# The norms between phases from three running sums, with GpSimd renewing half of the residual stream

## The chip, the cores and the metric

The kernel runs on one core of one Trainium2 chip. The metric is device time in microseconds (us) of the whole launch. The kernel before takes 2228.94 us, the median of 3 runs (2228.55 to 2229.42).

The engines by the names of the profile: PE is TensorE (PEld its weight loads), DVE is VectorE, ACT is ScalarE, POOL is GpSimd, SP is SyncE, which here only issues DMAs. A name with q behind it (SPq) is the queue of that engine.

## The reference

One inference step of a two-layer trunk over 384 tokens: 128 context tokens and 256 latent tokens (two groups with their own modulation vectors). Cut to what matters here:

```
def rmsnorm(x, g):
    xf = x * rsqrt(mean(x * x, axis=-1) + EPS)
    return xf * g

def trunk_layer(x, cond, ...):
    m = split(silu(cond) @ ada_w[l] + ada_b[l], 9)           # modulation, 9 x 1024
    h = rmsnorm(x, norm_pre[0]) * (1 + m[1]) + m[0]
    y = (silu(h @ wg) * (h @ wu)) @ wd                        # FFN, 1024 -> 2816 -> 1024
    x = x + 0.5 * m[2] * rmsnorm(y, norm_post[0])
    h = rmsnorm(x, norm_pre[1]) * (1 + m[4]) + m[3]
    y, _ = token_mixer(h, ...)                                # attention, recurrence, gates, @ w_out
    x = x + m[5] * rmsnorm(y, norm_post[1])
    h = rmsnorm(x, norm_pre[2]) * (1 + m[7]) + m[6]
    y = swiglu(h, ...)
    x = x + 0.5 * m[8] * rmsnorm(y, norm_post[2])
```

So between two products there are always two norms in a row: that of y (post), which makes the new x, and that of the new x (pre), which makes the next h. The places between are called gaps here. There are five of them inside the two layers, and one norm of y at the very end.

## The kernel before, in words

Everything is held with the 1024 features on the partitions, as 8 tiles (k = 0 to 7) of 128 features by 384 tokens, fp32. A sum over the features is therefore a product with a matrix of ones on PE (`ones`, the constant tile `con` in the rows), which leaves the sum of each token on all 128 partitions.

**Weights.** A unit is a block of 128x1024 fp32 weights (or 128x512). SP loads it into one of four `raw` slots (`stream`, L488). ACT copies it to `w_hi` (`highs`, L1028), POOL takes the rest of the rounding, `w_lo = raw - w_hi` (`lows`, L525, two instructions of 128x512), and PE does three products for each block: hi x hi, hi x lo, lo x hi (L588), 384 columns each. ACT and POOL work four units ahead of PE (SPLIT = 4). A `raw` slot is free for the next load when its low part is made; SP waits there in order (L485). A unit of kind "ada" (a slice of `ada_w`) is not split: PE multiplies it straight from the slot with the small `c_col` (`ada_unit`, L627).

**Phases.** A layer is up0, down0, gap0, proj and mixer, out, gap1, up1, down1, gap2. In a gap PE has up to 22 ada units to do (GAP = 22; the last gap, gap1 of layer 1, has 8). 18 of the 22 have places of their own (`hold_*`); numbers 14 to 17 go through the four `raw` slots, behind the first four weight units of the next phase. So number 17 is loaded when the low part of the fourth of these units is made. PE does all ada units of a gap before the first product of the next phase.

**The end of a phase.** y has four pairs of tiles, each pair in one PSUM pair X0 or X1. For each pair: ACT squares it (`y_square`, L1132, 128x768), DVE multiplies it by the column vector mG into `y` (`y_out`, L1601) and adds up the squares (L1606 to L1609).

**A gap.** PE sums the squares of y (`y_sums`, L696 to L699); ACT takes the square root (`root_of_sums`, L1088); DVE inverts it (L1560) and makes the new x in four steps (`post`: L1563 multiplies, L1565 and L1568 add); ACT squares each tile of x (L1110), PE sums them (`x_sums`, L705), ACT takes the root, DVE inverts it (L1538), and multiplies each tile (`pre`: L1527, L1532); ACT rounds to `h_hi` (L1117), DVE takes the rest, `h_lo` (`low`, L1518), and PE begins its products tile by tile (`by_tiles`).

Everything is ordered by semaphores that the code writes out by hand; each engine runs its instructions in the order of the code. There is no scheduler.

## Time and profile before

| | |
|---|---|
| time, median of 3 runs | 2228.94 us |
| the profiled execution, first to last instruction | 2228.5 us |
| PE busy | 2145.9 us (96%) |
| POOL busy | 1240.8 us (56%) |
| DVE busy | 915.8 us (41%) |
| ACT busy | 903.4 us (41%) |
| DMA | 311.37 MB, mean 140 GB/s |
| mean granted PE clock | 0.989 |

The profiled execution's own time is its span of 2228.5 us; 0.4 us separate it from the median, so what is worked out in one holds for the other. The page gives each group of instructions as: line, engine, operation, out<-in, shapes, count, busy us and mean ns of one, then the idle time before them and who ended it. A PE row of 0.33 us is one product whose next one starts 0.17 us later, since products are pipelined.

### The profile page before, as it was taken

Reading aid. Unit: us, or ns where it says so; the run is one execution under the profiler, and the core shown is the slowest. Engines: PE = TensorE matmul, PEld = TensorE weight load, DVE = VectorE, ACT = ScalarE, POOL = GpSimd, SP = SyncE. Lnnn points to the kernel's source line nnn. Section 1 sums busy time; section 2 is a strip of 40 time slices with the busy share of each in tenths; the row PEclk is TensorE's granted clock in tenths of the full one; section 3 lists DMA queues with packets and bytes.
Section 4 is the critical chain, followed back from the end, with each engine's and each line's share of the span. In section 5 each row is a group of like instructions: output and inputs, shape, how many; then the busy total and the mean of one; then the engine's idle time right before and its main releaser. Section 6 shows DMA issues by size and latency. Waiting matters only on the chain.

```text
span 2228.5 us, 32128 instructions
## 1 busy us (share of the span) xinstructions
PE 2145.9 (96%) x13212; PEld 2022.6 (91%) x13212; DVE 915.8 (41%) x1486; ACT 903.4 (41%) x1269; POOL 1240.8 (56%) x972
## 2 busy tenths in 40 slices
PE   6999999999899999999999999999999899899998
PEld 4999997988898988999979999799888899799997
DVE  5122116446766465121251221534576664622122
ACT  3222323246765534223243232324567546432332
POOL 2666553444478464666646666354435955366663
PEclk8999999999999999999999999999999999899999
DMA  7555674433222384445554446552322235244431
GB/s 282 160 163 172 224 237 162 124 88 95 67 86 86 109 297 117 129 133 171 193 185 124 138 124 234 194 152 87 87 78 76 86 114 176 61 136 128 124 123 67
DMA packets 306921, 311.37 MB, mean 140 GB/s; under 512 B 9923, under 2 KB 285655, under 8 KB 306775
## 3 DMA queue, kind: packets, MB, share of 16 engines
q1 hardware_dynamic: 299671, 303.55, 43.4%
q10 hardware_dynamic: 7104, 5.77, 0.8%
q8 instruction: 104, 1.70, 0.3%
q14 instruction: 42, 0.34, 0.1%
HBM read 305.35 MB, written 3.93 MB: 139 GB/s over the span
## 4 chain that ended last, share of the span: by engine, by line
PE 73%; DVE 12%; ACT 8%; POOL 3%; issue 2%; DMA 1%; SPq 0%; DVEq 0%; ACTq 0%
PE X L588 56%; PE S L588 6%; PE Ab L588 4%; POOL w_lo L525 2%; PE S L705 1%; ACT w_hi L1028 1%; POOL dec L553 1%; POOL dec L552 1%; PE X L766 1%; PE S L795 1%; ACT p L1181 1%; DVE mg_lo L1453 1%; DVE gate_b L1464 1%; PE X L848 1%; DVE root L1560 1%
## 5 line engine op out<-in xcount | busy, mean ns | idle before, releaser
L525 POOL TENSOR_TENSOR w_lo<-raw,w_hi 128x512 fp32r<-128x512 f32 (+1 forms) x872 | 1163.6, 1356 | 947.2 <-ACT w_hi L1028 938.2
L1028 ACT ACTIVATE w_hi<-raw 128x1024 fp32r<-128x1024 f32 (+1 forms) x436 | 453.3, 1041 | 723.6 <-PE X L588 687.7
L588 PE MATMUL X<-h_hi,w_hi 128*128 128x384 f32 x1600 | 539.7, 337 | 12.6 <-DVE h_lo L1518 12.6
L588 PE MATMUL X<-h_lo,w_hi 128*128 128x384 f32 x1600 | 536.8, 335 | 0.0
L588 PE MATMUL X<-h_hi,w_lo 128*128 128x384 f32 x1600 | 536.6, 335 | 0.0
L588 PEld LDWEIGHTS X<-h_hi,w_hi 128*128 128x128 f32 x1600 | 302.0, 189 | 24.5 <-DVE h_lo L1518 15.9
L588 PEld LDWEIGHTS X<-h_lo,w_hi 128*128 128x128 f32 x1600 | 302.0, 189 | 0.0
L588 PEld LDWEIGHTS X<-h_hi,w_lo 128*128 128x128 f32 x1600 | 301.9, 189 | 0.0
L1590 DVE TENSOR_TENSOR prod<-X,silu 128x768 f32<-128x768 f32 x44 | 42.1, 957 | 566.7 <-PE X L588 566.7
L588 PE MATMUL X<-act_hi,w_hi 128*128 128x384 f32 x704 | 236.4, 336 | 0.0
L588 PE MATMUL X<-act_hi,w_lo 128*128 128x384 f32 x704 | 235.3, 334 | 0.0
L588 PE MATMUL X<-act_lo,w_hi 128*128 128x384 f32 x704 | 235.3, 334 | 0.0
L1601 DVE TENSOR_SCALAR y<-X,mG 128x128 f32<-128x128 f32 x96 | 33.5, 411 | 340.7 <-ACT prod L1132 340.7
L588 PE MATMUL S<-h_hi,w_hi 128*128 128x384 f32 x480 | 166.5, 347 | 0.4 <-DVE proj L1432 0.4
L588 PE MATMUL S<-h_lo,w_hi 128*128 128x384 f32 x480 | 161.4, 336 | 0.0
L588 PE MATMUL S<-h_hi,w_lo 128*128 128x384 f32 x480 | 161.2, 336 | 0.0
L588 PEld LDWEIGHTS X<-act_hi,w_hi 128*128 128x128 f32 x704 | 132.1, 188 | 4.5 <-issue 4.5
L588 PEld LDWEIGHTS X<-act_lo,w_hi 128*128 128x128 f32 x704 | 132.2, 188 | 0.0
L588 PEld LDWEIGHTS X<-act_hi,w_lo 128*128 128x128 f32 x704 | 132.2, 188 | 0.0
L588 PE MATMUL Ab<-h_hi,w_hi 128*128 128x384 f32 x320 | 111.7, 349 | 0.7 <-DVE acc_e L1440 0.7
L588 PE MATMUL Ab<-h_hi,w_lo 128*128 128x384 f32 x320 | 107.3, 335 | 0.0
L588 PE MATMUL Ab<-h_lo,w_hi 128*128 128x384 f32 x320 | 107.2, 335 | 0.0
(364 smaller groups left out, 3075.3 us busy)
## 6 DMA issues: line engine op xcount, KB each, us to landing
raw<-in_w_in SPq DMA_DIRECT2D x124, 512.0 KB, 3.8
raw<-in_ffn_gate SPq DMA_DIRECT2D x88, 512.0 KB, 3.8
raw<-in_ffn_up SPq DMA_DIRECT2D x88, 512.0 KB, 3.7
raw<-in_ffn_down SPq DMA_DIRECT2D x80, 512.0 KB, 3.5
raw<-in_ada_w SPq DMA_DIRECT2D x48, 512.0 KB, 3.9
hold<-in_ada_w SPq DMA_DIRECT2D x29, 512.0 KB, 5.2
first_w<-in_ada_w SPq DMA_DIRECT2D x16, 512.0 KB, 10.6
hold_a<-in_ada_w SPq DMA_DIRECT2D x16, 512.0 KB, 6.4
```

Source lines behind the costliest of these rows:

```text
L525: ins = nc.gpsimd.tensor_tensor(slot(w_lo, u)[:, part], raw_of(u)[:, part], slot(w_hi, u)[:, part], SUB)
L552: nc.gpsimd.tensor_tensor(dst[:, :, 0:b], mid, src[:, :, 0:b], SUB)
L553: nc.gpsimd.tensor_tensor(dst[:, :, b:], src[:, :, b:], mid, SUB).then_inc(S["dec_ready"], 1)
L588: mm = nc.tensor.matmul(dst, w[:, k, m * 128:m * 128 + 128], r_, start=start and k + j == 0, stop=stop and k == u.nk - 1 and j == 2)
L705: mm = nc.tensor.matmul(S5[:, 0:T], ones, sq[:, k, :], start=k == 0, stop=k == KT - 1)
L766: mm = nc.tensor.matmul(X[n % 2][:, c, at_:at_ + k.shape[-1]], proj[64 * c:64 * c + 64, (AQ if kind == "a" else CQ) + h, b * 128:b * 128 + ...
L795: mm = nc.tensor.matmul((S5, S6)[c][:, 0:128], v, pT[:, c, j * 128:j * 128 + 128], start=j == 0, stop=j == len(kbs) - 1)
L848: mm = nc.tensor.matmul(X[0][:, j // 3, j % 3 * 128:j % 3 * 128 + 128], lev_k[n % 2][:, t], lev_q[n % 2][:, t], start=True, stop=True)
L1028: A(slot(w_hi, u), raw_of(u), ACT.Copy).then_inc(hi_ready[u.split], 1)
L1181: e = A(p[n % 2][:, c, 0:w], X[n % 2][:, c, 0:w], ACT.Exp, bias=nmax[:, n % 2, c:c + 1], accum_out=esum[:, n % 2, c:c + 1])
L1590: V.tensor_tensor(prod[:, :, :], X[1][:, :, 0:T], silu[:, :, :], MUL).then_inc(x_free[1], 1)
L1601: ins = V.tensor_scalar(y[:, 2 * i + m, t0:t1], X[u.dest][:, m, t0:t1], mG[:, 2 * i + m, g:g + 1], None, MUL)
```

## The change

While a phase's y tiles come out of PE, three sums over the features are built up instead of one: of the squares of the raw y (a), of x times the scaled y called g (b), and of the squares of g (c). With r = 1/sqrt(a/1024 + eps), the sum of the squares of the new x = x + r g is the old sum of x squared, plus 2 r b, plus r r c. So the norm of the new x is known before the new x is. The old sum is kept in `x_sum`.

- **Phase end**: `y_squares` (ACT) and `y_out` (DVE) go tile by tile: ACT squares the tile from PSUM, DVE makes g, ACT squares g, DVE multiplies x by g, adds that product to `y_sum`, and adds both squares to `silu[:, 0:2]` (one instruction of 768). The next tile's square on ACT waits for that last addition (`y_added`). The last pair is taken half by half (`half_done`).
- **Gap on PE**: three ada units, then three sums with ada units between them, then the rest of the ada units, then the products.
- **Gap on ACT**: an inverse root is now Ln and Exp (with a load of the function table between) in place of Sqrt on ACT and the reciprocal on DVE.
- **Gap on DVE**: `joint` makes the new `x_sum` in five dependent instructions, renews x tiles 0, 3, 6 and 7, and makes each normed tile with one instruction per token group (x times mA times the inverse root) where there were two.
- **Gap on POOL**: `add_to_x` renews x tiles 1, 2, 4 and 5 (four multiplications and four additions of 128x384). The high and low part of the fourth weight unit of the next phase, which stood before the gap, now stand behind: on ACT behind the first inverse root, on POOL behind `add_to_x`.
- At the start and at the very end the inverse root or root is Ln and Exp too.

```diff
@@ block.gpsimd
+            def add_to_x():
+                pool.wait_ge(S["root_ready"], 2 * seen.next("gap"))
+                for n, k in enumerate((*POOL_TILES, None)):
+                    if k is not None:
+                        nc.gpsimd.tensor_tensor(y[:, k, :], y[:, k, :], root[:, :], MUL).then_inc(S["y_pool_ready"], 1)
+                    if n:
+                        k = POOL_TILES[n - 1]
+                        pool.wait_ge(S["y_pool_ready"], seen.next("y_pool_ready"))
+                        nc.gpsimd.tensor_tensor(x[:, k, :], x[:, k, :], y[:, k, :], ADD).then_inc(S["x_pool_ready"], 1)
...
-                for f in range(2):
-                    lows(END[L, f"down{f}"] + SPLIT)
...
+                lows(END[L, "down0"] + SPLIT - 1)
+                add_to_x()
+                lows(END[L, "proj"] + SPLIT)
@@ block.tensor
             def gap(units):
-                y_sums()
-                early = 12 if len(units) > 12 else len(units) // 2
-                for u in units[:early]:
+                for u in units[:3]:
                     ada_unit(u)
-                x_sums([])
-                for u in units[early:]:
+                part_sum(S5[:, 0:T], silu[:, 0, :]).then_inc(S["sum_ready"], 1)
+                ada_unit(units[3])
+                pe.wait_ge(x_free[0], seen.value(("xf", 0)) + 1)
+                part_sum(X[0][:, 0, 0:T], y_sum[:, :])
+                ada_unit(units[4])
+                part_sum(X[0][:, 1, 0:T], silu[:, 1, :]).then_inc(S["sum_ready"], 1)
+                for u in units[5:]:
                     ada_unit(u)
@@ block.scalar
-            def root_of_sums():
+            def root_of_sums(power):
                 act.wait_ge(S["sum_ready"], seen.next("sum_ready"))
-                A(root[:, :], S5[:, 0:T], ACT.Sqrt, bias=eps[:, 0:1], scale=1.0 / D).then_inc(S["root_ready"], 1)
+                A(root[:, :], S5[:, 0:T], ACT.Ln, bias=eps[:, 0:1], scale=1.0 / D).then_inc(S["act_step"], 1)
+                act.wait_ge(S["act_step"], seen.next("act_step"))
+                A(root[:, :], root[:, :], ACT.Exp, scale=power).then_inc(S["root_ready"], 1)
...
+                        A(prod[:, 0, :] if k else silu[:, 0, :], X[u.dest][:, m, 0:T], ACT.Square).then_inc(S["y_sq_ready"], 1)
+                            act.wait_ge(S["g_made"], seen.next("g_made"))
+                            A(prod[:, 1, :] if k else silu[:, 1, :], y[:, k, :], ACT.Square).then_inc(S["c_made"], 1)
@@ block.vector
+            def joint(units):
+                def add_to_x(k):
+                    step(V.tensor_tensor(y[:, k, :], y[:, k, :], root[:, :], MUL))
+                    step(V.tensor_tensor(x[:, k, :], x[:, k, :], y[:, k, :], ADD))
+                dve.wait_ge(S["root_ready"], seen.next("root_ready"))
+                dve.wait_ge(S["sum_ready"], 2 * seen.next("gap") + 1)
+                step(V.tensor_tensor(part[:, :], X[0][:, 1, 0:T], root[:, :], MUL))
+                step(V.scalar_tensor_tensor(part[:, :], X[0][:, 0, 0:T], 2.0, part[:, :], MUL, ADD))
+                step(V.tensor_tensor(part[:, :], part[:, :], root[:, :], MUL))
+                step(V.scalar_tensor_tensor(part[:, :], x_sum[:, :], -1.0, part[:, :], MUL, ALU.max))
+                V.tensor_tensor(x_sum[:, :], x_sum[:, :], part[:, :], ADD).then_inc(S["x_sum_made"], 1)
+                add_to_x(0)
+                dve.wait_ge(S["root_ready"], seen.next("root_ready"))
+                dve.wait_ge(S["ada_used"], units[2].n + 1)
+                for k in range(KT):
+                    if k in POOL_TILES:
+                        dve.wait_ge(S["x_pool_ready"], seen.next("x_pool_ready"))
+                    for g, (t0, t1) in GROUPS:
+                        ins = V.scalar_tensor_tensor(sq[:, k, t0:t1], x[:, k, t0:t1], mA[:, k, g:g + 1], silu[:, 0, t0:t1], MUL, MUL)
+                    ins.then_inc(S["norm_ready"], 1)
+                    if k in (0, 3, 4):
+                        add_to_x({0: 3, 3: 6, 4: 7}[k])
...
+                def with_x(k):
+                    step(V.tensor_tensor(part[:, :], x[:, k, :], y[:, k, :], MUL))
+                    return V.tensor_tensor(y_sum[:, :], y_sum[:, :], part[:, :], ADD)
+                def added(k):
+                        step(V.tensor_tensor(silu[:, 0:n, :], silu[:, 0:n, :], prod[:, 0:n, :], ADD))
+                        dve.sem_inc(S["y_added"], 1)
```

How POOL's instructions stand at the first gap. Before, with the low parts of the third and fourth unit of the next phase, and then the fifth:

```order
L525 TENSOR_TENSOR w_lo<-raw,w_hi 128x512 [waits hi_ready2]
L525 TENSOR_TENSOR w_lo<-raw,w_hi 128x512
L525 TENSOR_TENSOR w_lo<-raw,w_hi 128x512 [waits hi_ready3]
L525 TENSOR_TENSOR w_lo<-raw,w_hi 128x512
L525 TENSOR_TENSOR w_lo<-raw,w_hi 128x512 [waits hi_ready0]
```

And of the change, in the same place (L566 multiplies, L570 adds to x):

```order
L529 TENSOR_TENSOR w_lo<-raw,w_hi 128x512 [waits hi_ready2]
L529 TENSOR_TENSOR w_lo<-raw,w_hi 128x512
L566 TENSOR_TENSOR y<-y,root 128x384 [waits root_ready]
L566 TENSOR_TENSOR y<-y,root 128x384
L570 TENSOR_TENSOR x<-x,y 128x384 [waits y_pool_ready]
L566 TENSOR_TENSOR y<-y,root 128x384
L570 TENSOR_TENSOR x<-x,y 128x384 [waits y_pool_ready]
L566 TENSOR_TENSOR y<-y,root 128x384
L570 TENSOR_TENSOR x<-x,y 128x384 [waits y_pool_ready] x2
L529 TENSOR_TENSOR w_lo<-raw,w_hi 128x512 [waits hi_ready3]
L529 TENSOR_TENSOR w_lo<-raw,w_hi 128x512
```

The low part that raises `lo_ready3` has moved behind eight new instructions and behind the wait for the inverse root. SP's order is the same in both kernels; this is its piece for that gap in the changed one, where the last load of `ada_w` (number 17) waits for `lo_ready3`:

```order
L492 DMA raw_53<-in_ada_w 128x1024 [waits lo_ready0]
L492 DMA hold_a_65<-in_ada_w 128x1024 [waits unit_done0] x2
L492 DMA raw_53<-in_ada_w 128x1024 [waits lo_ready1]
L492 DMA hold_a_65<-in_ada_w 128x1024 [waits unit_done1]
L492 DMA raw_53<-in_ada_w 128x1024 [waits lo_ready2]
L492 DMA raw_53<-in_ada_w 128x1024 [waits lo_ready3]
L492 DMA raw_53<-in_w_in 128x4x256 [waits ada_used] x4
```

Nothing moved here; what moved is the event that its last `ada_w` row waits for. On ACT the same gap was:

```order
L1132 ACTIVATE prod<-X 128x768 [waits sum_ready,y_added,unit_done3]
L1028 ACTIVATE w_hi<-raw 128x1024 [waits unit_done3,loaded3]
L1088 ACTIVATE root<-S,eps 128x384 [waits sum_ready]
L1110 ACTIVATE sq<-x 128x384 [waits x_ready,ada_used]
L1110 ACTIVATE sq<-x 128x384 [waits x_ready] x7
L1088 ACTIVATE root<-S,eps 128x384 [waits sum_ready]
```

and is now, from the square of the last tile but one (L1162 squares y, L1166 squares g):

```order
L1162 ACTIVATE prod<-X 128x384 [waits y_added,half_done]
L1166 ACTIVATE prod<-y 128x384 [waits g_made]
L1162 ACTIVATE prod<-X 128x384 [waits y_added,unit_done3]
L1166 ACTIVATE prod<-y 128x384 [waits g_made]
L1106 ACTIVATE root<-S,eps 128x384 [waits sum_ready]
L1108 ACT_TABLE_LOAD
L1108 ACTIVATE root<-root 128x384 [waits act_step]
L1047 ACTIVATE w_hi<-raw 128x1024 [waits unit_done3,loaded3]
L1116 ACT_TABLE_LOAD
L1116 ACTIVATE silu<-x_sum,eps 128x384 [waits x_sum_made]
L1118 ACT_TABLE_LOAD
L1118 ACTIVATE silu<-silu 128x384 [waits act_step]
```

The eight squares of x have gone, three table loads have come, and the high part of the fourth unit stands behind the first inverse root.

## Rows read from the trace of the kernel before

**Rows 1.** Page: the chain that ended last, shares by engine.
```profile
PE 73%; DVE 12%; ACT 8%; POOL 3%; issue 2%; DMA 1%; SPq 0%; DVEq 0%; ACTq 0%
```

**Rows 2.** Chain of waits through gap2 of layer 0: start us, us, what.
```profile
1124.27 0.82 ACT prod L1132
...
1125.13 0.91 PE S L698 x2
...
1126.72 0.59 ACT root L1088
...
1127.40 2.56 DVE root L1560
...
1145.10 4.95 PE X L588 x27
```

**Rows 3.** Two gaps: span, busy PE, PEld, DVE, ACT, POOL, PEclk, DMA share, GB/s.
```profile
1124.20:1145.10 20.90, 18.14 (x199) 8.96 (x198) 18.17 (x30) 8.21 (x16) 4.20 (x4) 1.00 0.43 138
...
1911.80:1934.30 22.50, 14.43 (x87) 7.07 (x85) 18.14 (x30) 8.21 (x16) 2.50 (x2) 0.83 0.17 47
```

**Rows 4.** Timeline of gap2: fourth unit's low part, load 17, ada units 16 to 21.
```profile
1126.10 2.51 POOL L525 TENSOR_TENSOR w_lo<-raw,w_hi 128x512 fp32r<-128x512 f32 x2 [0.21 <-ACT w_hi L1028]
...
1128.64 0.33 SPq L488 DMA_DIRECT2D raw<-in_ada_w  x1
...
1141.19 1.05 PE L627 MATMUL S<-raw,c_col 128*32 128x256 f32 x16
1142.05 1.91 PE L627 MATMUL S<-hold_a,c_col 128*32 128x256 f32 x32
```

**Rows 5.** Chain of waits in down0 of layer 0: a load, then products.
```profile
264.57 3.76 DMA raw<-in_ada_w
269.01 8.53 PE X L588 x48
```

**Rows 6.** Timeline, same phase: a load of an ada unit and its use.
```profile
293.49 0.33 SPq L488 DMA_DIRECT2D raw<-in_ada_w  x1
...
297.79 0.64 PE L627 MATMUL S<-raw,c_col 128*32 128x256 f32 x8
```

**Rows 7.** Timeline: DVE and POOL side by side, then POOL by itself.
```profile
804.38 1.16 DVE L1606 TENSOR_TENSOR y_sum<-prod 128x384 f32<-128x384 f32 x1
803.84 2.86 POOL L525 TENSOR_TENSOR w_lo<-raw,w_hi 128x512 fp32r<-128x512 f32 x2 [0.88 <-ACT w_hi L1028]
...
807.36 2.53 POOL L525 TENSOR_TENSOR w_lo<-raw,w_hi 128x512 fp32r<-128x512 f32 x2 [0.67 <-ACT w_hi L1028]
```

**Rows 8.** Groups over the span: count, busy us, mean ns, idle before.
```profile
L1532 DVE TENSOR_TENSOR sq<-y,root 128x384 f32<-128x384 f32 x40 | 21.6, 550 | 0.2
L1563 DVE TENSOR_TENSOR y<-y,root 128x768 f32<-128x768 f32 x20 | 19.0, 952 | 0.2
L1601 DVE TENSOR_SCALAR y<-X,mG 128x128 f32<-128x128 f32 x96 | 33.5, 411 | 340.7 <-ACT prod L1132 340.7
L553 POOL TENSOR_TENSOR dec<-b_f 128x384 f32<-128x384 f32 x24 | 21.6, 900 | 0.0
```

**Rows 9.** Timeline: Ln, table load and Exp in the mixer.
```profile
498.19 1.90 ACT L1079 ACTIVATE c_rt<-c_rt,eps 128x1920 f32<-128x1920 f32 x1
500.11 1.28 ACT L1083 ACT_TABLE_LOAD   x1
501.40 1.81 ACT L1083 ACTIVATE c_rt<-c_rt 128x1920 f32<-128x1920 f32 x1
```

**Rows 10.** PE around gap1 of layer 1; in brackets its idle time before.
```profile
1920.31 8.44 PE L705 MATMUL S<-sq,con 128*128 128x384 f32 x16 [4.13 <-ACT sq L1110]
...
1935.15 0.53 PE L588 MATMUL X<-h_hi,w_lo 128*128 128x384 f32 x1
...
1940.19 0.33 PE L588 MATMUL X<-h_hi,w_hi 128*128 128x384 f32 x1
```

**Rows 11.** Chain of waits at the start: the first inverse root.
```profile
24.81 2.56 DVE root L1499
```

More of the change, by code:

```diff
@@ L121, in build @@
     ada_t, o = at("ada_t", [128, 256], f32, o)
+    part, o = at("part", [128, T], f32, o)
     assert o <= Y_END
@@ L246, in build @@
         lo_ready = [sem(f"lo_ready{s}") for s in range(SPLIT)]
-        first_in = [sem(f"first_in{n}") for n in range(16)]
         unit_done = [sem(f"unit_done{s}") for s in range(SPLIT)]
@@ L655, in stream @@
                         mm = product(X[u.dest][:, m, 0:T], u, m, u.k0, u.first, u.last)
+                        if m == 0 and u.last and u.tag == ("y", 3):
+                            mm.then_inc(S["half_done"], 1)
                     mm.then_inc(unit_done[u.split], 1)
@@ L1347, in _ @@
                 root_table()
-                stream(PHASES[L, "down0"], {"y": y_square})
-                gap(PHASES[L, "gap0"])
+                stream(PHASES[L, "down0"], {"y": y_squares(15 * L + 1, True)})
+                gap(PHASES[L, "gap0"], END[L, "down0"] + SPLIT)
                 mixer_loads(L)
@@ L1353, in _ @@
                 root_table()
-                stream(PHASES[L, "out"], {"y": y_square})
-                gap(PHASES[L, "gap1"])
+                stream(PHASES[L, "out"], {"y": y_squares(15 * L + 14, True)})
+                gap(PHASES[L, "gap1"], END[L, "out"] + SPLIT)
                 silu_table()
@@ L1412, in stream @@
                     if u.last and u.tag[0] in outputs:
-                        dve.wait_ge(unit_done[u.split], u.split_turn + 1)
+                        if u.tag == ("y", 3):
+                            dve.wait_ge(S["half_done"], seen.next("half_done"))
+                        else:
+                            dve.wait_ge(unit_done[u.split], u.split_turn + 1)
                         outputs[u.tag[0]](u, u.tag[1])
@@ L1498, in first_pre @@
                 dve.wait_ge(S["root_ready"], seen.next("root_ready"))
-                step(V.reciprocal(root[:, :], root[:, :]))
                 first = [u for u in PHASES["first"] if u.last]
@@ L1513, in first_pre @@
                     low(k)
+                V.tensor_copy(x_sum[:, :], S5[:, 0:T])
             def low(k):
@@ L1555, in post_factors @@
                     step(V.tensor_scalar(mG[:, :, :], mG[:, :, :], 0.5, None, MUL))
-            def post():
+            def joint(units):
+                def add_to_x(k):
+                    step(V.tensor_tensor(y[:, k, :], y[:, k, :], root[:, :], MUL))
+                    step(V.tensor_tensor(x[:, k, :], x[:, k, :], y[:, k, :], ADD))
                 dve.wait_ge(S["root_ready"], seen.next("root_ready"))
-                step(V.reciprocal(root[:, :], root[:, :]))
-                for c in range(4):
-                    t = slice(2 * c, 2 * c + 2)
-                    step(V.tensor_tensor(y[:, t, :], y[:, t, :], wide(root[:, :], 2), MUL))
-                    if c < 3:
-                        V.tensor_tensor(x[:, t, :], x[:, t, :], y[:, t, :], ADD).then_inc(S["x_ready"], 2)
-                    else:
-                        for k in (2 * c, 2 * c + 1):
-                            V.tensor_tensor(x[:, k, :], x[:, k, :], y[:, k, :], ADD).then_inc(S["x_ready"], 1)
-                dve.wait_ge(S["x_ready"], seen.next("my_x", KT))
+                dve.wait_ge(S["sum_ready"], 2 * seen.next("gap") + 1)
[15 more added lines that the diff above has]
+                        add_to_x({0: 3, 3: 6, 4: 7}[k])
+                    dve.wait_ge(S["norm_ready"], seen.next("my_norm"))
+                    if k:
+                        low(k - 1)
+                low(KT - 1)
@@ L1978, in _ @@
                 post_factors(L, 1)
-                stream(PHASES[L, "out"], {"y": y_out()}, factors(L, 1))
-                post()
-                pre()
+                stream(PHASES[L, "out"], {"y": y_out(True)}, factors(L, 1))
+                joint(PHASES[L, "gap1"])
                 take_groups(PHASES[L, "gap1"])
```

172 lines of the change are left out of this document (91 added, 81 removed).

## The prediction

> **What bounds the kernel now.** I read the chain of waits by engine first. PE is 73% of it [rows 1] and is busy 96% of the span, so little can be won outside the places where PE stands. Then I read the chain through one gap [rows 2]: the last product ends at 1124.2, the first of the next phase starts at 1145.1, and between them lie a square on ACT, two sums on PE, a root, and twice a reciprocal of 2.56 us on DVE. The gap is 20.9 us long, with DVE busy 18.2 us of it [rows 3]; the other three gaps with 22 ada units have the same length. The gap with 8 units takes 22.5 us, at a mean clock of 0.83 [rows 3]. Last I read what else passes through a gap: POOL makes the fourth unit's low part from 1126.1 to 1128.6, SP starts ada load 17 at 1128.64, as that part ends, and PE needs it at about 1141.6, the second of the two units in the row of 1141.19 [rows 4]. That load has 9 us to spare. It is not seen in the chain, and it decides the forecast.
>
> The first error to avoid is to count only the arithmetic: two reciprocals (5.1 us), eight squares of x with their sums, and the four-step renewal of x leave the chain, some 17 of 20.9 us, and what replaces them looks shorter.
>
> **Prices.** E is the end of a phase's last product.
> - DVE, two operands, 384 columns: 0.55 us; 768 columns 0.95 us [rows 8]. A hop between engines or a dependent step adds 0.06 to 0.1. The scaled copy g is two instructions of 0.41 on average [rows 8], overlapping to 0.7.
> - ACT: 0.8 us for the square of 768 columns, 0.6 us for a root of 384 [rows 2]. I take 0.5 for a square and an Exp of 384.
> - PE: a sum 0.9 us [rows 2]; an ada unit 0.43, half the distance between the starts of 1141.19 and 1142.05 [rows 4].
> - POOL: 512 columns 1.25 us (half of the 2.53 for two), 384 columns at most 0.90 by the row of L553, whose inputs are repeated values [rows 7, 8]. By columns it would be 0.94. I take 0.95.
> - DVE beside POOL: at 804.38 an addition of two SBUF tiles of 384 takes 1.16 us instead of 0.55. It starts inside POOL's first instruction (1.25 us from 803.84, so until about 805.1) and ends 0.42 after that. POOL's pair then takes 2.86 instead of 2.53 [rows 7]. So each waits for the other's whole instruction. When both have a queue they alternate, and DVE pays POOL's instruction for each of its own.
>
> The Trainium skill states this as a rule (SBUF — State Buffer, section SBUF: two separate sides): the pair of ports that DVE and GpSimd share is an exclusive lock for the whole instruction. The trace agrees, with the 1.16 us above. The rule speaks against this change, which puts eight POOL instructions beside DVE work on SBUF tiles.
>
> **A gap with 22 units behind a down phase (3 of them).**
> 1. E to the first inverse root. The half that holds tile 6 ends 1.0 before E: square to -0.5, g to +0.2. The product x times g then waits for POOL, which makes the third unit's low part until about +1.5: +1.9. Its addition to +2.5, the addition of 768 to +3.5, and only then ACT's square of tile 7, to +4.1. g to +4.8, sum of squares to +5.3, PE's sum to +6.3, Ln to +6.9. Ln and Exp have different tables: the load is 1.28 and Exp follows at once [rows 9], so +8.7. Before, the inverse root stood at E+5.7 (1129.96 less 1124.2) [rows 2].
> 2. POOL's eight instructions start there, and DVE begins `joint`. Its first two instructions read PSUM and are out of it; from the third on (`x_sum`, tile 0, the normed tile 0) all have two SBUF operands. Eight times 0.95, plus the part that each DVE instruction in between needs once POOL lets go (five of 0.42, one of 128 columns at 0.15), less the starts that overlap (about 0.06 each): 9.4. Now +18.2.
> 3. The fourth unit's low part: two of 1.2, with two more DVE instructions in between: 3.0, so +21.2.
> 4. Load 17 starts there: 3.76 to landing [rows 5], so +25.0.
> 5. Ada units 17 to 21, before the first product: 2.2, so **+27.2**. Against 20.9: **+6.3**.
>
> DVE's own path is not later: x_sum at +13.7, Ln, load, Exp to +16.2, normed tile 0 to +18.4, x tile 3 to +21.6, normed tile 1 and h_lo 0 to +23.2. The tiles behind keep ahead of PE's 2.1 us a tile.
>
> At 1. the Trainium skill has another price: ScalarE: Activation LUTs, section What ACT_TABLE_LOAD costs, gives 1.28 us and 1.38 of drain for each switch. Here Exp starts 0.01 us after the load ends [rows 9], so I add no drain. By the page, one switch more on this path would add 1.4 us a gap, 7 us in all.
>
> **The same gap behind the out phase (layer 0).** A pair of tiles is there every 8.3 us. The chain of a pair (step 1 twice, 3.7 each) plus the high parts that stand behind it on ACT, plus up to four waits for POOL, fills that. By the same steps, tile 6 is squared at +1.4 instead of -0.5, its products wait for the low parts of the second and third unit, and the inverse root stands at +12.5. POOL, load 17 and ada units follow as before: +30.9, **+10.0**. PE itself does not wait inside the out phase: I find the closest low part ready 2.6 us ahead.
>
> **The gap with 8 units (layer 1).** Load 17 does not exist. The inverse root at +12.5, DVE's path from there 14.5: h_lo 0 at +27.0 against 22.5; x tiles 6 and 7, now renewed between normed tiles, add 1.4 behind it: **+5.9**.
>
> **Clock.** In the gap with 8 units PE was idle for 4.13 us [rows 10], and its products began at the lower level (1.2 GHz): 16 products take the 5.04 us from 1935.15 to 1940.19 [rows 10]; at 0.178 each [rows 5] they take 2.8. The long gap shown holds 1.00 now [rows 3]. After the change PE is idle for 11 us before load 17 lands (+13.9 to +25.0). I take 2.3 us for each of the four: **+9.2**. Bounds: 0, and 3 with the ada units slowed too.
>
> **Elsewhere.**
> - down0 of layer 0 has eight ada units in the ring. On ACT the high parts at a pair's end now stand behind the whole tile chain, 5.7 us instead of 0.8. The load at 293.49 is used at 297.79, 0.5 after it lands [rows 5, 6]. It waits for such a part, which comes 4.9 later: **+4.2** (bounds 0 and 9, were a second load late too).
> - The very end: no x_sum, but the tile chain, then Ln, load and Exp: root at E+6.2 instead of E+3.1, all of it bare: **+3.1**.
> - The start: Ln, load and Exp (2.4) for root and reciprocal (0.59 and 2.56 [rows 2, 11]): **-0.7**.
> - The dropped squares of x, and h products: nothing is added to PE's 2146 us but a few sums.
>
> Sum: 3 x 6.3 + 10.0 + 5.9 + 9.2 + 4.2 + 3.1 - 0.7 = 50.6. The profiled execution has 2228.5, so 2279.1; the median is 0.4 above it. I say **2279 us**.
>
> **Rivals.**
> - *No alternation*: DVE and POOL share the ports without loss. Speaks against it: rows 7. Then the inverse root stands at +7.6, POOL ends at +15.3, the low part at +17.8, and the gap at +23.8, so +2.9 three times, +4.5 behind out, -2 in the gap of 8; clock +8, end 3, start -0.7, down0 +2: 9 + 4 + 8 + 4 = 25, **2253 us**. 0.15.
> - *The out phases back up*: if each of a pair's six SBUF instructions meets POOL, 7.4 + 4 x 1.25 = 12.4 us against 8.3, ACT's high parts are late by 4 us a pair and PE waits. Three pairs in two phases: 24 more, **2303 us**. For it: 60% of POOL's time there is taken. Against: ACT is four units ahead. 0.12.
> - *Load 17 is hidden after all, and the lock is mild*: products start with h_lo 0, at E+16.8 without any lock; 1.6 lost again where x tiles 6 and 7 delay the following tiles: 18.4 against 20.9, 2.5 us won four times, end and down0 5 lost: **2224 us**, faster. It decides from the point where the fourth unit's low part ends before E+14.9, since 3.8 of load and 2.2 of ada units follow and 20.9 is the mark; without any lock it ends at +17.8. For it: the load had 9 us to spare. Against: the order on POOL puts eight instructions before it. 0.05.
>
> **Chances and range.** 0.68 for the forecast, 0.15, 0.12 and 0.05 for the rivals. A measurement here tells 0.2% (4.5 us) from no change. Slower 0.94, same 0.02, faster 0.04. The range is 2252 to 2300: down to the first rival, up almost to the second, with the clock's and down0's bounds inside.
>
> **What the profile after would show.** In the long gaps the chain should read POOL add, POOL w_lo L529, DMA raw<-in_ada_w, ada units, product, about 27 us from last to first product, 31 behind out. DVE's `x_sum` instructions should take 1.3 us where they take 0.55 alone. PE's clock should read below 1 at the start of the phases. I am wrong if PE waits for DVE's h_lo in the long gaps, or if they are shorter than 21 us; or if PE waits for low parts inside the out phases.

## The result and the profile after

The changed kernel takes 2287.35 us (median; 2286.78 to 2288.59), the kernel before 2228.89 beside it: ratio 1.0263, 95% interval 1.0248 to 1.0277. The forecast was 2279, in a range of 2252 to 2300. The profiled execution's span grew from 2228.5 to 2286.8 us, by 58.3.

In the chain of waits by engine PE falls from 73% [rows 1] to 70, and POOL doubles, from 3% to 6:

```profile
PE 70%; DVE 12%; ACT 8%; POOL 6%; issue 2%; DMA 1%; SPq 0%; DVEq 0%; ACTq 0%
```

The chain through gap2 of layer 0, to be laid beside [rows 2] (start us, us, what). The last product ends at 1155.1, which is E:

```profile
1155.63 1.70 DVE part L1640
...
1160.91 0.93 PE S L703 x2
...
1163.75 0.53 ACT root L1108
...
1164.35 1.96 POOL y L566 x2
...
1170.79 2.54 POOL x L570 x2
1173.33 2.81 POOL w_lo L529 x2
1176.16 3.75 DMA raw<-in_ada_w
1179.95 4.50 PE S L645 x40
1184.45 1.65 PE X L606 x5
```

This is the chain that the prediction wrote down: inverse root, eight instructions on POOL (four multiplications, four additions), low part, load, ada units, product. The timeline of the same gap, on DVE, SP and PE (in brackets the idle time before and what ended it), answers to [rows 4]:

```profile
1168.69 1.24 DVE L1581 SCALAR_TENSOR_TENSOR part<-x_sum,part 128x384 f32<-128x384 f32 x1
1169.96 1.25 DVE L1582 TENSOR_TENSOR x_sum<-x_sum,part 128x384 f32<-128x384 f32 x1
...
1176.16 0.33 SPq L492 DMA_DIRECT2D raw<-in_ada_w  x1
1176.34 0.55 DVE L1572 TENSOR_TENSOR y<-y,root 128x384 f32<-128x384 f32 x1
...
1179.95 1.08 PE L645 MATMUL S<-raw,c_col 128*32 128x256 f32 x8 [8.42 <-DMA raw<-in_ada_w]
```

Load 17 starts at E+21.1, where it started 4.4 us after E before [rows 2, 4]; PE stands still for 8.42 us. DVE's steps to `x_sum` take 1.25 us beside POOL, and the same kind of step takes 0.55 as soon as POOL has finished.

Windows of that gap and of the one with 8 units (columns as in [rows 3]):

```profile
1155.10:1184.40 29.30, 16.63 (x184) 7.00 (x183) 24.01 (x40) 12.50 (x21) 13.58 (x12) 0.79 0.53 190
1960.60:1990.60 30.00, 9.38 (x72) 3.27 (x71) 23.42 (x33) 12.14 (x18) 17.24 (x14) 0.73 0.17 51
```

POOL's time in the long gap went from 4.20 [rows 3] to 13.58 us, DVE's from 18.17 to 24.01 though its reciprocals are gone, and the granted clock from 1.00 to 0.79.

Between the last product of a phase and the first of the next, and in down0 of layer 0, in us, all read from the start times of the products (the prediction's 20.9 us and its E for the kernel before were read 0.1 us apart from these):

| kernel | L0 gap0 | L0 gap1 | L0 gap2 | L1 gap0 | L1 gap1 (8 units) | down0 of L0 |
|---|---|---|---|---|---|---|
| before | 21.0 | 21.0 | 21.0 | 21.0 | 22.7 | 99.3 |
| changed | 30.1 | 35.1 | 29.3 | 30.4 | 30.1 | 107.2 |
| k1_low_first | 22.9 | 28.2 | 22.2 | 23.2 | 27.8 | 107.1 |
| k2_no_pool | 20.5 | 24.6 | 20.6 | 20.8 | 24.6 | 106.7 |
| k3_pool_adds | 24.3 | 24.3 | 24.3 | 24.3 | 24.3 | 99.5 |
| k4_ln_exp | 19.5 | 19.5 | 19.5 | 19.5 | 21.0 | 99.9 |
| k10_clock13 | 28.1 | 33.5 | 28.1 | 28.1 | 30.1 | 105.8 |
| k9_one_set | 18.3 | 18.3 | 18.3 | 18.3 | 17.9 | 99.6 |

The changed kernel's five gaps are 48.3 us longer together, down0 7.9, the end 2.8, and the start is 0.8 shorter: 58.2 of the 58.3. (The start is the time up to the first product.)

### The profile page after: what moved, and what is told of

Read it like the earlier page. It is cut to its first block, busy times and chain, and to the rows that moved or that the text cites. A ratio compares the mean times of both kernels' runs of the same rounds, so it can differ in the third digit from the quotient of the medians.

```text
span 2286.8 us, 32207 instructions
## 1 busy us (share of the span) xinstructions
PE 2139.7 (94%) x13128; PEld 2012.7 (88%) x13128; DVE 964.0 (42%) x1548; ACT 933.8 (41%) x1320; POOL 1290.8 (56%) x1012
## 4 chain that ended last, share of the span: by engine, by line
PE 70%; DVE 12%; ACT 8%; POOL 6%; issue 2%; DMA 1%; SPq 0%; DVEq 0%; ACTq 0%
PE X L606 54%; PE S L606 5%; PE Ab L606 4%; POOL w_lo L529 2%; PE S L645 1%; DMA raw<-in_ada_w 1%; ACT w_hi L1047 1%; POOL dec L557 1%; POOL dec L556 1%; PE X L785 1%; POOL x L570 1%; POOL y L566 1%; PE S L814 1%; ACT p L1216 1%; DVE mg_lo L1492 1%
## 5 line engine op out<-in xcount | busy, mean ns | idle before, releaser
L606 PEld LDWEIGHTS X<-h_lo,w_hi 128*128 128x128 f32 x1600 | 302.3, 189 | 0.0
L606 PE MATMUL Ab<-h_lo,w_hi 128*128 128x384 f32 x320 | 107.2, 335 | 0.0
```

Of the source, the lines that this page charges most:

```text
L606: mm = nc.tensor.matmul(dst, w[:, k, m * 128:m * 128 + 128], r_, start=start and k + j == 0, stop=stop and k == u.nk - 1 and j == 2)
```

## Experiments

Each was timed against the kernel before on the same chip (2230.1, 2230.0 and 2230.8 us in the three groups, 2228.9 beside the changed kernel). Ratios are to that kernel, with their 95% interval. Small differences between groups are taken from the ratios.

### k1_low_first: the fourth unit's parts back before the gap

```diff
-                        if u.tag != ("y", 3) or not u.last:
-                            highs(u.n + SPLIT + 1)
+                        highs(u.n + SPLIT + 1)
...
-                lows(END[L, "down0"] + SPLIT - 1)
+                lows(END[L, "down0"] + SPLIT)
```

(and the same for out and down1.)

> The changed kernel with the fourth weight unit's high and low part back in front of the gap, on ACT and on POOL. Theory (ada load 17 waits for that low part behind POOL's adds, and the first product waits for load 17): the load lands by about E+13.5, long before its turn, and PE's last wait in the long gaps turns to DVE's h_lo, at about E+24 behind a down phase and E+30 behind the out phase of layer 0. The gaps shrink from 29.3 to 30.4 and 35.1 us to about 24.5 and 31, part of it is given back by tiles that now come late and by the clock: 2270 to 2277 us. The gap with 8 units does not change. Rival (the load only looks like the last event, and DVE's path stands just behind it): within 4 us of 2287.

Measured 2264.73 us, 1.0159 (1.0143 to 1.0174): 22.6 less than the changed kernel. The last part of the chain in gap2, with E at 1144.5:

```profile
1158.79 1.25 DVE x_sum L1581
...
1161.36 1.26 DVE x L1572
...
1166.69 3.39 PE X L606 x18
```

POOL's low part, load 17 and the ada units have left the chain, as steps 3 to 5 of the prediction require, and the gap fell by 7.1 us. What ends it now is DVE, in steps of 1.25 to 1.3 us beside POOL. PE's stop before the first product is 3.59 us long where the stop before the ada units was 8.42, and the granted clock over this gap is 0.92 where it was 0.79.

The gain is above the range that was expected. The five gaps are 30.8 us shorter together, but the products and mixers behind them take 7 us more. The expectation gave two reasons, late tiles and the clock; the trace shows the clock. Behind gap1 of layer 0, for example, PE has stood still for 3.13 us, and its first 18 products start 0.32 us apart instead of 0.17: the phase's first run of products takes 186.7 us for 184.0. Once the first product has started, PE waits for no tile. Over the five gaps such slow starts cost 5.8 us more than in the changed kernel. One part of the expectation missed: the gap with 8 units has no load 17 and should have kept its length, but it fell by 2.3 us. The low part of the fourth unit stood on POOL beside the first normed tile there, too: that tile's pair of instructions on DVE takes 1.35 us here and took 2.62. The other 1.0 is in PE's sums and the ada units between them, which ran at a higher granted clock here.

Of the change's 58 us, 34.6 are left: 17.5 in the five gaps, 7.8 in down0 of layer 0, 3.1 at the end, 7 in the products and mixers behind the gaps, less 0.9 at the start. No run takes those in down0 and at the end away.

### k2_no_pool: DVE renews all eight tiles

```diff
-        POOL_TILES = (1, 2, 4, 5)
+        POOL_TILES = ()
...
-                add_to_x()
...
-                    if k in (0, 3, 4):
-                        add_to_x({0: 3, 3: 6, 4: 7}[k])
...
                     if k:
                         low(k - 1)
+                        if k + 1 < KT:
+                            add_to_x(k + 1)
```

(`add_to_x()` without a tile is POOL's, with a tile DVE's. The rest is k1_low_first.)

> As k1_low_first, and DVE renews all eight tiles of x itself, two before the second inverse root and one behind each h_lo; POOL does nothing in a gap but the low part. Theory (DVE and POOL lock each other out of SBUF instruction by instruction): x_sum's three SBUF instructions fall from 1.25 to 0.55 us, the first h_lo comes at about E+19 instead of E+24, and although DVE now has 8 renewals of 1.2 us and falls behind PE (h_lo every 2.7 us against 2.1), the phase starts no later than in k1_low_first: 2262 to 2272 us. Rival (POOL takes real work off DVE and costs it nothing): 4 more renewals of 1.2 us behind each gap's start, so 10 to 20 us slower than k1_low_first.

Measured 2272.94 us, 1.0196 (1.0181 to 1.0212): 8 us above k1_low_first, between the two expectations, and both hold in part. In the gap the theory is right. The last step to `x_sum` is short again:

```profile
1160.77 0.57 DVE x_sum L1577
```

and the long gaps behind down phases take 20.5 to 20.8 us. But DVE's work for a tile behind the gap (renewal 1.1, scaled copy 0.7, low part 0.7) is then longer than PE's products for it, and PE waits inside the phase. The window of the products of up1, of this kernel and of the kernel before:

```profile
1166.50:1357.10 190.60, 186.93 (x1064) 184.23 (x1064) 52.33 (x72) 59.35 (x68) 118.14 (x86) 0.99 0.43 126
```

```profile
1145.10:1329.10 184.00, 184.00 (x1064) 183.14 (x1064) 44.58 (x60) 59.37 (x68) 118.14 (x86) 1.00 0.44 130
```

The same 1064 products take 6.6 us more. The five runs of products behind a gap pay 28 us together (58.3 for 51.6 twice, 189.3 for 183.9, 190.6 for 184.0, 188.5 for 185.8), and the group of PE's products by `h_hi` shows for whom it waits (last column; it was 12.6 us before). By the start times of the products, 24 of the 28 us are such waits and 4 are products at the lower clock:

```profile
L602 PE MATMUL X<-h_hi,w_hi 128*128 128x384 f32 x1600 | 543.9, 340 | 32.6 <-DVE h_lo L1552 31.5 <-DVE proj L1682 1.1
```

So DVE has no room for all of x either, and giving half to POOL is worth 8 us at this place. Even without POOL's turns, the scheme of three sums makes a long gap behind a down phase only 0.2 to 0.6 us shorter than before, and the one behind the out phase of layer 0 is 3.6 longer.

### k3_pool_adds: the kernel before, with half of x renewed by POOL

```diff
-                for c in range(4):
...
-                    step(V.tensor_tensor(y[:, t, :], y[:, t, :], wide(root[:, :], 2), MUL))
...
+                dve.sem_inc(S["inv_ready"], 1)
+                for k in (0, 3, 6, 7):
+                    step(V.tensor_tensor(y[:, k, :], y[:, k, :], root[:, :], MUL))
+                    V.tensor_tensor(x[:, k, :], x[:, k, :], y[:, k, :], ADD).then_inc(S["x_ready"], 1)
```

(and POOL's `add_to_x` from the change, for tiles 1, 2, 4 and 5. To have semaphores for it, the first 16 loads share those of later ones; the first product starts at 40.6 us, where it started at 40.9.)

> The kernel before, with one part of the change alone: POOL multiplies and adds x tiles 1, 2, 4 and 5 in the gap, DVE tiles 0, 3, 6, 7; norms, sums and the low parts as before. Theory of the lock: both have 8 instructions with two SBUF operands and alternate, 1.3 to 1.4 us each pair, so x is complete after about 11 us instead of 8 and each of the five gaps grows by about 3: 2240 to 2248 us. Rival (no lock): DVE is done after 5, POOL after 8 us, no gap grows by more than 1: 2229 to 2233 us.

Measured 2244.52 us, 1.0067 (1.0052 to 1.0082): the lock's expectation, and outside the rival's. The groups over the span (count, busy us, mean ns, idle before), 20 instructions of each kind:

```profile
L1582 DVE TENSOR_TENSOR y<-y,root 128x384 f32<-128x384 f32 x20 | 27.2, 1359 | 0.7
L566 POOL TENSOR_TENSOR x<-x,y 128x384 f32<-128x384 f32 x20 | 25.9, 1305 | 0.0
L1583 DVE TENSOR_TENSOR x<-x,y 128x384 f32<-128x384 f32 x20 | 24.7, 1237 | 0.7
L562 POOL TENSOR_TENSOR y<-y,root 128x384 f32<-128x384 f32 x20 | 24.5, 1234 | 7.5 <-DVEq L1580 7.5
```

All four show the same step: one instruction of the one engine and one of the other take 1.3 us together, whichever record they stand in. DVE alone needs 0.95 for two tiles [rows 8]. Sixteen instructions shared by two engines end later than eight wide ones on DVE.

### k4_ln_exp: the kernel before, with the change's inverse root

```diff
-                A(root[:, :], S5[:, 0:T], ACT.Sqrt, bias=eps[:, 0:1], scale=1.0 / D).then_inc(S["root_ready"], 1)
+                A(root[:, :], S5[:, 0:T], ACT.Ln, bias=eps[:, 0:1], scale=1.0 / D).then_inc(S["act_step"], 1)
+                act.wait_ge(S["act_step"], seen.next("act_step"))
+                A(root[:, :], root[:, :], ACT.Exp, scale=power).then_inc(S["root_ready"], 1)
...
-                step(V.reciprocal(root[:, :], root[:, :]))
```

(Ln's table is loaded ahead of each gap and once more behind its first inverse root. The last root of the kernel stays Sqrt.)

> The kernel before, with one other part alone: the eleven inverse roots as Ln, table load and Exp on ACT in place of Sqrt on ACT and reciprocal on DVE; Ln's table is loaded ahead of each, behind other waits; the last root stays Sqrt. Theory (a switch costs the 1.28 us of its load and nothing else): 0.58 + 1.28 + 0.52 = 2.4 against 0.59 + 0.08 + 2.56 = 3.2 us, so 0.8 us won eleven times: 2219 to 2222 us. Rival (a switch costs 2.7 us, load and drain): 0.6 us lost eleven times: 2234 to 2237 us.

Measured 2221.49 us, 0.9964 (0.9950 to 0.9978), faster than both kernels. The chain in gap2:

```profile
1124.55 0.58 ACT root L1091
...
1125.15 1.28 ACT L1093
...
1126.44 0.53 ACT root L1093
```

The load of 1.28 us has nothing behind it: Exp starts 0.01 after it ends, and the long gap is 1.5 us shorter where 2.56 of reciprocal went twice. So the prediction was right to add no drain of 1.38 us for a switch: by the expectation's estimate, this kernel would have been slower than before with it.

### k5_clock and k10_clock13: TensorE kept busy before load 17

```diff
                 for u in units[5:17]:
                     ada_unit(u)
+                pe.wait_ge(S["root_ready"], 2 * seen.next("kept"))
+                if len(units) > 17:
+                    for _ in range(18):
+                        nc.tensor.matmul(S5[:, 0:T], ones, con[:, 0:T], start=True, stop=True)
```

(12 in k10_clock13. The rest is the changed kernel.)

> The changed kernel, with 18 extra products of TensorE (128x384, ones by a constant, written to the bank of the sums that nobody reads then) between conditioning units 16 and 17 of each gap with 22 units, where TensorE stands still for 8.4 us. No other engine's work changes. Theory (the 4.50 us of the last conditioning units, where 2.2 had been forecast, come from the clock, which fell to half during that stop): the granted clock stays full at the units, they take 2.0 to 2.4 us, and each of the four long gaps is 2 to 3 us shorter, with 0.3 to 0.6 less in the products behind three of them: 2275 to 2280 us against 2287.4. Rival 1: the half clock there doesn't come from the stop: 2286 to 2289. Rival 2: the extra products take the place of the units themselves (they end after load 17 has landed): 2287 to 2295.

Measured 2294.43 us, 1.0291 (1.0276 to 1.0307): 6 above the changed kernel by the ratios, as rival 2 had it, and the chain shows the reason that it gave:

```profile
1176.34 11.81 PE S L721 x36
1188.14 1.86 PE S L645 x31
```

Each of the 18 is recorded as two products, together 11.8 us, and they end 3.3 us after the load landed. The 40 products of the ada units behind them take 2.3 us (1.86 for the 31 that this row holds) where the changed kernel's took 4.50. Hence the second run.

> The changed kernel with 12 extra products of TensorE in place of the 18 of the run before (2294.4), in which they ran for 11.8 us and ended 3.3 us after load 17 had landed. 12 of them take 7.9 us at the full clock and should end at E+24.5, as the load lands (E+24.8), E being the end of the last product. Theory (the stop of 8.4 us lets the clock fall, and the last conditioning units pay for it): the units take 1.9 us as they did in the run with 18, where the changed kernel has 4.50, and the gap between layers is 26.6 to 27.2 us against 29.3; with 0.5 less in the products behind it, 2275 to 2279 us against 2287.4. Rival (the extra products delay load 17 or the low part that it waits for, and not their number was to blame): the units start at E+27 or later, 2286 to 2292.

Measured 2280.33 us, 1.0226 (1.0210 to 1.0241), 8 below the changed kernel by the ratios. The same gap, with E at 1149.8:

```profile
1155.62 1.66 PE S L703 x2
...
1171.82 3.71 DMA raw<-in_ada_w
...
1175.58 2.37 PE S L645 x40
```

The 40 products of the units take 2.37 us (as in k5_clock; the 1.9 of the expectation left out nine of them) and the granted clock over the gap is 0.94. So the half clock of these units came with the stop: fill the stop, and it is gone. The gain is less than expected (2280.3 for at most 2279) because load 17 comes at E+25.8 instead of E+24.8: the sum of squares at E+5.8 fell into a stretch at the lower level (1.66 us for 0.93), and root, POOL and load follow it.

### k6_factors: shifts and scales before the out phase's first unit

```diff
-                    if early and u.first and u.tag == ("y", 3):
+                    if early and u.first and u.tag == ("y", at):
...
-                stream(PHASES[L, "out"], {"y": y_out(True)}, factors(L, 1))
+                stream(PHASES[L, "out"], {"y": y_out(True)}, factors(L, 1), 0)
```

(`at` is a new argument of `stream`, 3 everywhere else.)

In the changed kernel these four instructions on 16 columns stand at the head of the chain in gap1 of layer 0 (E is 843.7; the first and the last of the four, and the root):

```profile
845.19 1.02 DVE mB L1519
...
848.68 1.20 DVE mA L1526
...
858.40 0.53 ACT root L1108
```

> The changed kernel, with the four small instructions that make the next norm's shifts and scales (128x16) before the first unit of the out phase instead of its fourth. Theory (beside GpSimd's low parts they take 4.6 us instead of 0.7, and the three sums of the out phase end that much later, as the inverse root at E+15.2 against the forecast of E+12.5 shows): both gaps behind an out phase are 3 to 4 us shorter, 2280 to 2282 us against 2287.4. Rival 1: VectorE is late in the out phase for its own eight sums, and takes the four with it wherever they stand: 2286 to 2288. Rival 2: the low part of the fourth unit and load 17 end the gap as before, since these hang on GpSimd, not on VectorE; as GpSimd's additions start by the inverse root, this holds only if the root is not earlier: 2287.

Measured 2285.37 us, 1.0251 (1.0234 to 1.0268), above the expected range: the two gaps behind an out phase are 1.5 and 1.7 us shorter, not 3 to 4. DVE and POOL in the same place (timeline, E is 843.9):

```profile
844.51 6.12 POOL L529 TENSOR_TENSOR w_lo<-raw,w_hi 128x512 fp32r<-128x512 f32 x4 [3.82 <-ACT w_hi L1047]
...
846.74 1.23 DVE L1640 TENSOR_TENSOR part<-x,y 128x384 f32<-128x384 f32 x1
848.01 1.50 DVE L1641 TENSOR_TENSOR y_sum<-y_sum,part 128x384 f32<-128x384 f32 x1
849.54 1.90 DVE L1648 TENSOR_TENSOR silu<-silu,prod 128x768 f32<-128x768 f32 x1
```

DVE comes to tile 6 four microseconds earlier, and now tile 6's three steps wait for POOL's low parts (4.6 us where they took 2.1). So most of the 4.6 us was lost again by other instructions: what DVE loses there hangs, as far as this one run shows, on how long POOL is busy more than on which instructions DVE has in line.

### k8_pool_late: POOL starts when x_sum is made

```diff
-                pool.wait_ge(S["root_ready"], 2 * seen.next("gap"))
+                pool.wait_ge(S["x_sum_made"], seen.next("gap"))
```

(The rest is k1_low_first.)

> The kernel with the fourth unit's parts back before the gap (2264.7), and GpSimd starts its eight additions only when the new sum of squares of x is made, about 4.5 us later. Theory (the two engines take turns at full length: VectorE's two last steps to the sum took 1.25 us each beside GpSimd against 0.57 alone): each gap ends 1.3 to 1.4 us earlier where the first tile's norm is what it waits for, and tiles 4 and 5 come 4.5 us later, which the products wait for at most 2 us of: 2259 to 2268 us. Rival (GpSimd's additions are not what slows VectorE's steps): no gap is shorter, the late tiles cost 2 to 4 us in each of five gaps: 2275 to 2285.

Measured 2277.59 us, 1.0216 (1.0201 to 1.0232): 13 above k1_low_first (all of it in the five gaps), in the rival's range, though the rival's reason is wrong. DVE in gap2 (timeline):

```profile
1162.64 0.56 DVE L1581 TENSOR_TENSOR x_sum<-x_sum,part 128x384 f32<-128x384 f32 x1
...
1165.79 2.29 DVE L1590 SCALAR_TENSOR_TENSOR sq<-x,mA,silu 128x128 f32<-128x128 f32 x2 [0.84 <-ACT silu L1117]
...
1170.64 2.09 DVE L1590 SCALAR_TENSOR_TENSOR sq<-x,mA,silu 128x128 f32<-128x128 f32 x2
```

`x_sum` takes 0.56 without POOL, which confirms the lock. Then POOL's eight instructions fall on the first normed tiles, whose pair of half-tile instructions takes 2.1 to 2.3 us instead of 0.75. Each half pays a whole POOL instruction.

### k9_one_set: one table set for Ln and Exp

```diff
             def root_table(last=False):
...
-                A(tick_a[:, :], eps[:, :], ACT.Sqrt if last else ACT.Ln)
+                if last:
+                    A(tick_a[:, :], eps[:, :], ACT.Sqrt)
+                    return
+                nc.scalar.add_instruction(mybir.InstLoadActFuncSet(
+                    act_func_set_id=6, name=nc.get_next_instruction_name(), engine=nc.scalar.engine, ins=[], outs=[]))
```

(The rest is k4_ln_exp, without its second load in each gap.)

> The kernel before with Ln and Exp for the inverse roots (2221.5), and in place of the table load that each function brings with it one load, ahead of the gap, of a set that holds both. Theory (the load of 1.28 us between Ln and Exp is all on the path, in both norms of each of five gaps and once at the start): 2.56 us less in each gap, 1.3 at the start, 2207 to 2210 us. Rival 1 (the load is placed by function all the same, or its wait was hidden): 2220 to 2222. Rival 2 (the clock of TensorE or the load of the silu table behind the gap takes part of it back): 2212 to 2217.

Three executions took 2207.83, 2209.18 and 2211.57 us; a fourth took 5435.65, for which no trace shows a reason, and is left out of the ratio: 0.9911 (0.9895 to 0.9928). It is the fastest kernel of this study. The end of the chain in gap2:

```profile
1133.36 1.86 PE Ab L627 x32
1135.22 2.59 PE S L627 x48
1137.81 1.26 PE X L588 x6
```

The time is in the expected range, but by luck in part: the loads are gone (58 in the whole kernel, 82 in k4_ln_exp), and yet the long gap lost 1.2 us against k4_ln_exp, not 2.6, since PE's ada units end it now. The gap with 8 units lost 3.1.

### k11_units_in_sums and k12_best: tries to go on from there

```diff
-                x_sums([])
-                for u in units[early:]:
+                among = units[early:early + (3 if len(units) > 12 else 1)]
+                x_sums(among)
+                for u in units[early + len(among):]:
```

(The rest is k9_one_set.)

> The kernel before with Ln and Exp out of one table set (2210.4), with three of TensorE's ten late conditioning units (one of four in the gap with eight) put between the sums of squares of x, which TensorE gets in pairs each 1.9 us. Theory (in the run before, each long gap became 1.24 us shorter where two loads of 1.28 had gone, because ten units of 0.44 us behind the last sum now end it): the gap falls from 18.3 to 17.0 to 17.3, 2205 to 2207 us. Rival 1 (the units delay the last pair's sum, which VectorE's path waits for): 2209 to 2212. Rival 2 (not the units, but the norm's tiles end the gap): 2210.

Measured 2213.85 us, 0.9928 (0.9914 to 0.9943): above all three ranges, and the long gap is 19.2 us where it was 18.3. The theory was wrong; what rival 1 feared came, and cost more than it said. PE is full, and the units among the sums only make the sums late:

```profile
1131.65 1.49 PE S L706 x4
1133.14 0.57 PE Ab L627 x8
```

A pair of sums takes 1.49 us and a unit 0.57, together 2.06, and DVE's pairs come every 1.9.

k12_best is this kernel with the same table set also loaded at two places in the mixer, ahead of the head roots' wait and of the decays' logarithms:

```diff
+                root_table()
                 act.wait_ge(S["o_sum_ready"], seen.next("o_sum_ready"))
...
+                    if n == 4:
+                        root_table()
```

> The kernel of the run before this one, and the set with both Ln and Exp loaded ahead of the two other places with a Ln and an Exp in a layer: the decays' logarithms beside the attention's Exp, and the root of the mixer's heads. Theory (these loads lie on the chain of waits: 1.28 at 561.59 and 564.39, and 1.26 behind the Ln at 760.82): three loads less and one moved ahead of its wait, 3 to 6 us in each of two layers: 2194 to 2201 us. Rival (the products of the fill or VectorE's scans take over as soon as ScalarE is earlier): 2202 to 2206.

Measured 2213.03 us, 0.9927 (0.9912 to 0.9941). The expectation missed: four loads of 1.28 us fewer in each layer's mixer (50 in the whole kernel, 58 in k11_units_in_sums) brought 0.8 us, within what the timing tells from nothing. The reason that the rival gave fits, though not its time: PE has work at both places anyway. In k11_units_in_sums it is busy 37.3 of the 40 us from 560 to 600, and 48.1 of the 50 from 750 to 800.

### k13_change_one_set: the same set in k1_low_first

The edit is that of k9_one_set, in `root_table` of k1_low_first, here for the last root too.

> The changed kernel with the fourth unit's parts back before the gap (2264.7), and its inverse roots out of one table set. Theory (the load between Ln and Exp is on the path of both roots there too, and the sum of squares of x ends the gap by VectorE's steps, taken in turns with GpSimd): 1.3 to 2.6 us less in each of five gaps: 2252 to 2258 us, so the scheme of three sums stays 40 us above what the same table set gives the kernel before (2210.4). Rival 1 (GpSimd then starts 1.3 us earlier, and its turns fall on other steps of VectorE, which takes the gain back): 2260 to 2265. Rival 2 (the scheme gains more from the set than the kernel before did): below 2250.

Measured 2260.90 us, 1.0136 (1.0118 to 1.0154): 4 to 5 less than k1_low_first, rival 1's range. The chain in gap2, with E at 1141.8:

```profile
1153.07 0.57 DVE part L1577
...
1158.68 1.25 DVE x L1573
```

That gap is 22.2 us as in k1_low_first. DVE's first joint step starts at E+11.2 in both, since it waits for PE's third sum and not for the root, and `x_sum`'s own root is back before DVE has renewed tile 0 in turns with POOL. Neither root is on the path of this gap any more. The profiled executions differ by only 1.7 us: the very end is 1.3 shorter, the first gap of layer 1 1.0 and the start 0.6, and the products give part of it back: behind gap2 of layer 0 the first ones now run at the lower clock, 2.0 us in all. Where the rest of the 4 to 5 us lies is open.

## Why the prediction was right

It was within 0.4%: slower by 50 was said, 58 came. By its steps, in gap2 of layer 0 with E at 1155.1:

| step | forecast | measured |
|---|---|---|
| 1. first inverse root | E+8.7 | E+9.2 |
| 2. POOL's eight instructions | 9.4 | 9.0 |
| 3. low part ends | E+21.2 | E+21.0 |
| 4. load 17 landed | E+25.0 | E+24.8 |
| 5. ada units 17 to 21 | 2.2 | 4.5 |
| first product | E+27.2 | E+29.3 |

Steps 2 to 4 are shown by k1_low_first, in which the low part and load 17 vanish from the chain and 7.1 us from the gap, and the turns of DVE and POOL behind step 2 by k3_pool_adds and k8_pool_late. This agrees with the Trainium skill's rule that the prediction weighed (SBUF — State Buffer, section SBUF: two separate sides), with 1.3 us for a pair of instructions here.

That the total came within 8 us is in part luck: the clock term, 9.2 us, was right in size and laid on the wrong instructions. The terms that were mis-sized:
- **Clock.** 2.3 us for each long gap was the right size at the wrong place: step 5 took 2.3 more than forecast. I laid it on the first products, by [rows 10]; it is in step 5, which the bounds named, and the products paid at most 0.6. Where the long stop is gone (k1_low_first) and PE waits 3 us for h_lo, they do pay: 2.5 us behind gap1 of layer 0. k10_clock13, in which step 5 takes 2.37, shows the cause: the stop of 8.4 us.
- **Out phase, layer 0.** Inverse root at E+15.2, not E+12.5. The prediction's step did not hold the four instructions of the next norm's factors, which stand before tile 6 on DVE and cost 4.6 us there. k6_factors shows that moving them gives back only 1.5: tile 6's steps then wait for POOL's low parts. The prediction counted waits for POOL by instruction; POOL's busy time at that place would have been the better measure.
- **Gap with 8 units.** +7.4 for +5.9, for the same reason: its first inverse root stands at E+15.3, not E+12.5, and moving the four instructions gives back 1.7. DVE's path from there took 14.7 for 14.5. The 1.4 for tiles 6 and 7 behind the gap did not come; the products there took 0.8 less than before.
- **down0 of layer 0.** +7.9 for +4.2. The load and the stop of PE came as written (4.42 us; the prediction's own 4.9 less 0.5 is 4.4, not 4.2):

```profile
298.54 3.71 DMA raw<-in_ada_w
...
302.28 1.08 PE S L645 x8
303.37 10.89 PE X L606 x48
```

  But the 48 products behind the stop ran at the lower level for part of their time, 10.89 us against 8.53 [rows 5]: the granted clock is 0.50 from 302.3 to 305 us and 0.66 from 305 to 310. I had put a clock cost on the gaps and none on this stop. No run tests it.
- **End and start.** +2.8 and -0.8 for +3.1 and -0.7.

The rivals: without alternation the gaps would have been near 24 us; they are 29 to 30, and k3_pool_adds excludes it. (Its terms add up to 23.5 us, not to 25: 4.5 less 2 is 2.5, where the sum has 4.) The out phases did not back up: their products take 35.4 us before and after. Load 17 was not hidden.

The rule that decides k9_one_set is in the Trainium skill as well (ScalarE: Activation LUTs, section Table sets: the hidden batching unit): one set holds both functions, and Ln with Exp needs one load. In the change a load of 1.28 us stood before each of the two, as nothing named the joint set, and the pair took 2.4 us; with the set named (k9_one_set) it takes 1.1, as the page has it.

## What to carry to other kernels

Before an engine is given work beside another, look for what that engine already does in the same stretch and what hangs on it: here POOL's eight instructions cost 14 us by themselves (k3_pool_adds), less than the weight part and the load queued behind them (of the 58 us, 23 went with k1_low_first). Where VectorE and GpSimd both read two SBUF tiles, count the pair as one engine that takes turns. Splitting elementwise work between them cost 14 us where DVE by itself was done with it sooner (k3_pool_adds). It gained 8 where DVE was full behind the gap and POOL could begin while DVE stood still (k1_low_first against k2_no_pool; in the changed kernel POOL's first two instructions run in DVE's idle 3.9 us). And try the parts of a change apart: the inverse root by Ln and Exp alone was worth 8 to 9 us, with one table set 20.

## What the hardware showed that I had not expected

- The wait for POOL does not shrink with DVE's instruction: one of 128x16 took 1.0 to 1.2 us beside POOL's low parts and 0.17 alone, about what 128x384 took (1.2). Among them was a TENSOR_SCALAR with a single tile as input.
- TensorE's granted clock fell to its lower level (0.50 of full speed, 1.2 GHz) around the stops of 4.42 us in down0 and 8.42 us in the long gaps, and what ran then took up to twice as long: ada units 4.50 for 2.3 us, a sum 1.66 for 0.93. With filler products in the long stop it was at the upper level (2.4 GHz) for most of the gap (0.94 over it, where it was 0.79).
- The table load between Ln and Exp can be saved by naming the set, and nothing drained behind a load: Exp starts 0.01 us after it ends (k4_ln_exp).
